# Joint attention: the scores of two heads as 256-column pieces in turns, where each head had its 512 and its 256 columns in one go

## What is computed

```
def diff_attention(q, k, v, lam, lam_init, subln_g):
    s = jnp.einsum('bqhid,bkhid->bhiqk', q, k) * (HEAD_DIM ** -0.5)
    p = jax.nn.softmax(s.astype(jnp.float32), axis=-1)
    attn = (p[:, :, 0] - lam * p[:, :, 1]).astype(v.dtype)
    o = jnp.einsum('bhqk,bkhe->bqhe', attn, v)
...
def gqa_attention(q, k, v):
...
    s = jnp.einsum('bqgrd,bkgd->bgrqk', q, k) * (HEAD_DIM ** -0.5)
    p = jax.nn.softmax(s.astype(jnp.float32), axis=-1).astype(v.dtype)
    o = jnp.einsum('bgrqk,bkgd->bqgrd', p, v)
```

## Time and profile before

| | |
|---|---|
| times of three executions | 2624.16, 2630.66, 2631.01 us |
| median | 2630.66 us |
| span of the profiled execution (first to last instruction) | 2627.9 us |
| PE busy | 2557.7 us, 97% of the span |
| PE weight loads | 2102.4 us, 80% |
| DVE, ACT, POOL busy | 1581.3, 1048.3, 258.4 us |
| attention jobs 0 to 31 | 1489.5 to about 1640 us of the span |
| score matmuls (L3002) | 256 passes, 2% of the chain that ended last |

### The profile page before, as it was taken

One profiled execution on the slowest core, in us unless ns is written; L12 is line 12 of the kernel. 1 busy time (PEld: TensorE's weight loads), 2 busy tenths in 40 slices (PEclk: granted clock), 3 DMA queues, 4 the chain that ended last, 5 costly groups with the idle time before them and its releaser, 6 DMA issues.

```text
span 2627.9 us, 37789 instructions
## 1 busy us (share of the span) xinstructions
PE 2557.7 (97%) x13070; PEld 2102.4 (80%) x13070; DVE 1581.3 (60%) x2460; ACT 1048.3 (40%) x1663; POOL 258.4 (10%) x187
## 2 busy tenths in 40 slices
PE   8999999999999999999989999999999999999997
PEld 6887788888877778888878776788888888888886
DVE  6764665656578866565665786655555665644445
ACT  5334522223347852222353266553223522522333
POOL 2320100000320010000030100310000301300002
PEclk9999999999999999999999999999999999999999
DMA  3221344444320034444432100234444243332222
GB/s 133 73 88 65 118 137 144 144 145 151 135 73 25 26 113 144 144 144 144 144 121 73 41 1 1 81 112 144 144 149 140 96 144 116 104 100 96 96 96 80
DMA packets 79337, 277.46 MB, mean 106 GB/s; under 512 B 8448, under 2 KB 11904, under 8 KB 78720
## 3 DMA queue, kind: packets, MB, share of 16 engines
q1 hardware_dynamic: 58560, 205.55, 23.6%
q10 hardware_dynamic: 20672, 70.51, 8.1%
HBM read 273.92 MB, written 2.10 MB: 105 GB/s over the span
## 4 chain that ended last, share of the span: by engine, by line
PE 85%; DVE 8%; ACT 3%; issue 2%; DMA 1%; POOL 1%; ACTq 0%; DVEq 0%; SPq 0%; POOLq 0%
PE banks L2425 64%; PE banks L2566 5%; PE banks L3002 2%; PE banks L2469 2%; DVE w_lo L1403 1%; PE banks L2944 1%; PE banks L2600 1%; PE banks L2876 1%; DMA w_raw<-weights 1%; PE banks L2853 1%; PE banks L2956 1%; ACT w_hi L679 1%; PE banks L2973 1%; DVE nsa_e L1968 1%; PE banks L2838 1%
## 5 line engine op out<-in xcount | busy, mean ns | idle before, releaser
L679 ACT ACTIVATE w_hi<-w_raw 128x1024 fp32r<-128x1024 f32 x367 | 386.4, 1053 | 621.5 <-PE banks L2425 514.9
L2425 PE MATMUL banks<-h_hi,w_hi 128*128 128x512 f32 x1600 | 628.2, 393 | 1.1 <-DVE w_lo L1403 0.7
L2425 PE MATMUL banks<-h_hi,w_lo 128*128 128x512 f32 x1600 | 623.4, 390 | 0.0
L2425 PE MATMUL banks<-h_lo,w_hi 128*128 128x512 f32 x1600 | 623.2, 389 | 0.0
L1403 DVE TENSOR_TENSOR w_lo<-w_raw,w_hi 128x1024 fp32r<-128x1024 f32 x367 | 474.2, 1292 | 108.7 <-ACT w_hi L679 92.1
L2425 PE MATMUL banks<-g_hi,w_hi 128*128 128x512 f32 (+1 forms) x1108 | 427.7, 386 | 9.8 <-DVE w_lo L1403 8.8
L2425 PE MATMUL banks<-g_lo,w_hi 128*128 128x512 f32 (+1 forms) x1108 | 423.9, 383 | 0.0
L2425 PE MATMUL banks<-g_hi,w_lo 128*128 128x512 f32 (+1 forms) x1108 | 423.7, 382 | 0.0
L2425 PEld LDWEIGHTS banks<-h_hi,w_hi 128*128 128x128 f32 x1600 | 300.5, 188 | 66.5 <-issue 2.8
L2425 PEld LDWEIGHTS banks<-h_lo,w_hi 128*128 128x128 f32 x1600 | 300.6, 188 | 62.8 <-issue 1.7
L2425 PEld LDWEIGHTS banks<-h_hi,w_lo 128*128 128x128 f32 x1600 | 300.4, 188 | 62.9
(11 more groups left out here) (411 smaller groups left out, 3290.8 us busy)
## 6 DMA issues: line engine op xcount, KB each, us to landing
w_raw<-weights SPq DMA_DIRECT2D x384, 512.0 KB, 3.3
ada_raw<-ada ACTq DMA_DIRECT2D x112, 512.0 KB, 3.3
nsa_bias<-nsa_bias ACTq DMA_DIRECT2D x6, 512.0 KB, 3.4
x<-x SPq DMA_DIRECT2D x4, 512.0 KB, 6.6
out<-x SPq DMA_DIRECT2D x8, 256.0 KB, 2.1
mix_cum<-ret_tab ACTq DMA_DIRECT2D x1, 1024.0 KB, 4.7
rows_c<-c_rows ACTq DMA_DIRECT2D x1, 1024.0 KB, 5.6
nsa_w<-cmp_w ACTq DMA_DIRECT2D x1, 1024.0 KB, 5.4
```

Of the source, the lines that this page charges most:

```text
L679: act.activation(w_hi[s][:], w_raw[s][:], ACT.Copy).then_inc(w_hi_done, 1)
L2425: mm = pe.matmul(bank, w[s][:, k, :], m[:, k, :], start=(n == 0 and a == 0), stop=(n == kts - 1 and a == 2))
```

## The change

The scores of a head come as three matmuls of 256 columns where they came as one of 512 and one of 256, and the heads take turns: piece 0 of b0, piece 0 of b1, piece 1 of b0, and so on. Banks, columns, operands and semaphore counts are as before: pieces 0 and 1 go into the first bank of a head, piece 2 into its second. The wait of b1 now stands behind piece 0 of b0.

```
-                    for b in range(2):
-                        if j:
-                            pe.wait_ge(a_exp, 2 * j + b - 1)
-                        rows = slice(64 * b, 64 * b + 64)
-                        q = B2["aq" if j < 16 else "bq"][rows, m, qi * P:(qi + 1) * P]
-                        keys = B2["ak"][rows, m, :] if j < 16 else B2["bk"][rows, m // 2, :]
-                        for a, (c0, c1) in enumerate(((0, T), (T, NK))):
-                            mm = pe.matmul(banks[:, 2 + 2 * b + a, 0:c1 - c0], q, keys[:, c0:c1], start=True, stop=True)
-                        mm.then_inc(a_s, 1)
+                    for c0 in range(0, NK, CTX):
+                        for b in range(2):
+                            if j and c0 == 0:
+                                pe.wait_ge(a_exp, 2 * j + b - 1)
+                            rows = slice(64 * b, 64 * b + 64)
+                            q = B2["aq" if j < 16 else "bq"][rows, m, qi * P:(qi + 1) * P]
+                            keys = B2["ak"][rows, m, c0:c0 + CTX] if j < 16 else B2["bk"][rows, m // 2, c0:c0 + CTX]
+                            mm = pe.matmul(banks[:, 2 + 2 * b + c0 // T, c0 % T:c0 % T + CTX], q, keys, start=True,
+                                           stop=True)
+                            if c0 + CTX == NK:
+                                mm.then_inc(a_s, 1)
```

## The result

The changed kernel takes 2632.43 us (median of 17 runs, 2629.04 to 2636.49), the kernel before 2628.28 us in the 17 runs beside it (2624.14 to 2631.12). The ratio is 1.0019, 95% interval 1.0013 to 1.0025: slower by 5.0 us, between 3.4 and 6.6 (the two medians lie 4.2 apart).

A forecast was written before the change was run, and what follows sets the result against it. PE, busy 97% of the span, was taken to bound the kernel. Delays of 1.2 (jobs 4 to 17), 0.5 (job 1) and 0.2 (job 18) sum to +1.9 us on 2630.66, giving 2632.5; range 2626.5 to 2637.5.

The forecast's parts named there:

- stage A: Attention jobs 2 to 17, where b0's scores lie on the loop; mean period before 4.165 us over jobs 4 to 17.
- o: Distance in a job from b0's first weight load to b1's; in stage A before, it alternated 0.63 and 0.41 us.
- o(next) = 1.03 - o + d: Stage A: the next job's o from this one's; d is the delay of b0's end, which goes into it.
- stage B: Attention jobs 18 to 31, whose loop leaves b0 out; b0's maximum has 0.8 us to spare, forecast cost 0.
- The rival of a gain from pairing the heads: Attention scores: heads didn't run side by side before and turns make them; -23 us, about 2608; chance 0.04.
- The rival of loads that exclude each other: Attention scores: a weight load keeps out the other half's; +19 us, 2650; chance 0.05.
- The released pieces: b0's pieces 1 and 2, behind b1's wait: they stream 0.13 us after release, bounds 0.11 and 0.33.
- The wait of b1 moved up: PE's in-order queue holds b0's pieces 1 and 2 behind b1's wait, delaying b0's end by max(0, o - 0.41).
- 14 jobs, +1.2: Jobs 4 to 17 in stage A: period 4.25 us against 4.165, +1.2 us in all.
- Job 1, +0.5: Attention start: o = 0.88 delays b0's end by 0.47 in job 1, and job 2 with it; +0.5 us.
- a rival with chance 0.08: The clock: a half-clock stretch comes (up to 3.5 us) or goes (less than 3.5); chance 0.08, either way.
- Job 18, +0.2: Job 18 gets o = 0.62 where it had 0.41, and job 19 starts on a wait for ACT; +0.2 us.

The follow-up runs named there:

- Turns of 512: Against the change, heads take turns with the old sizes, b0 512, b1 512, b0 256, b1 256; ratio to the kernel before 1.0010.
- hold only: Against the change, all of b0's 256-column pieces ahead of b1's, but b1's wait in front of b0's second piece; ratio to the kernel before 1.0015.
- wait-late order: The change with b1's first piece and its wait one piece later (b0 b0 b1 b0 b1 b1); ratios to the kernel before 1.0007 and 0.9996.
- second set of runs: The changed kernel, unaltered, timed and profiled once more against the kernel before; ratio 1.0017 (1.0008 to 1.0027).

## Why the prediction was right, and where it was not

**Right: the class and the direction, and the loops.** The change stays within 0.3%. In stage A o stands at 0.62, the period at 4.25, the maximum of b0 at 1.87, all as worked out from o(next) = 1.03 - o + d; stage B has d = 0.06 and its old period. The rival of a gain from pairing the heads is out: they were paired before. The rival of loads that exclude each other is out too: in the change both halves load within 0.01 of each other from b1's release on in every job from 1 on, and the turn stays 1.49 behind b1. The released pieces came as forecast: b0's next load stands 0.01 behind b1's, near the lower bound, and the maximum moved by o - 0.41.

**Right number, half the reason: "The wait of b1 moved up", d = max(0, o - 0.41).** The prediction knew only the hold. The completion order gives the same start of the maximum, o + 0.11 + 4 x 0.215 + 0.27 = o + 1.24, because b1's first two pieces are as long as the two pieces that b0 still has to do. Turns of 512 show the second cause without the first, hold only the first without the second. Either suffices; taking one away would have gained nothing. Only the wait-late order removes both.

**Mis-sized: the sum of +1.9 us.** Profiled are +3.5 in the attention, timed +5.0 (3.4 to 6.6). The terms, one by one:
- *14 jobs, +1.2:* the periods were right, but d = o - 0.41 has a consequence that I didn't draw. With o(next) = 1.03 - o a job that is late makes the next o smaller by as much, and the lateness is given back. With d growing as o does, o(next) is 0.62 whatever o was, and nothing is given back. ACT's late exponential in job 8 and the end of the stretch at the lower clock (o = 0.01 in job 4, 0.88 in job 5) each cost 0.27 (jobs 9 and 5, period 4.52). Jobs 5 to 17 took 4.153 each before (59.67 - 5.68 = 53.99 over 13), so 4.25 in all of them gives +1.3, and +0.2 at job 18 makes 1.5. The two late jobs account for the difference to the 2.03 measured. The late job 8 was there before too, but there it was given back (o = 0.63 in job 9, 0.41 in job 10).
- *Job 1, +0.5:* measured 0.47. What follows it was missing: +0.9 with the longer stretch at the lower clock, which I had only as a rival with chance 0.08 and priced at up to 3.5. A stretch that came or went in the attention was among the prediction's own signs of being wrong, and one grew from 6.8 to 10.2.
- *Job 18, +0.2, stage B, 0:* measured 0.2 (5.89 for 5.68) and 0.05.

**"Cutting 512 in two costs no time by itself"** was right for this change and wrong as a rule: in stage B it costs 0.07 a job when the whole of b0 stands before b1, because b1 is then handed out late.

What stays open: the timed loss is 1.5 us larger than the profiled one at the middle of its interval. 3.5 lies within that interval and within that of the second set of runs, 2.1 to 7.1 us. From the first load of job 31 to the end of the span both profiles of the change take 1.1 us more than those of before, 997.4 against 996.2 and 996.3. A stretch at half clock near 2256 us is 6.8 there instead of 3.4. The other kernels need 995.8 to 998.9 for that part, so this may be chance.

## What to carry to other kernels

When independent matmul streams share the array, look at their first loads before mixing them by hand: if the second stream already starts when its own input is ready, mixing has nothing to gain. A wait belongs behind as much of the other stream as lasts until it is usually met, and a matmul that raises a semaphore belongs ahead of the other stream's long ones, since it is reported only when they are through. And where two engines chase each other with an alternating offset, ask what a change does to the giving back of a late start, not only to the mean.

## What the runs showed of the hardware

- An f32 pass costs 0.84 ns a column at 2.4 GHz in pieces of 256 or 512 alike (0.43 and 0.215 us a pass), and two halves of 64 rows run at full rate beside each other, weight loads included: in the change they load within 0.01 us of each other and b1's turn comes 1.49 behind its first load, where it was 1.48.
- Starts cross the program order between the halves: b1's second load, at 1577.01, comes ahead of b0's last, at 1577.40. Completions as a semaphore sees them don't: with turns of 512 b0's maximum started 0.2 us late behind b1's 512 columns, at 1.72, 1.86 and 2.13 for o = 0.47, 0.62 and 0.89.
- In these kernels PE handed out b1 past four pairs of load and matmul of b0 that hadn't finished (0.04 behind b0), but not past six (0.54).
